# Attention on one Trainium2 core: two score chunks of a unit next to each other in TensorE's order

## The chip, the cores and the metric

The kernel runs on one core of one Trainium2 chip. The metric is the time of one execution on the device, in microseconds (us). A core has five engines with a queue each: TensorE (PE; PEld are its weight loads), VectorE (DVE), ScalarE (ACT), GpSimd (POOL) and SyncE (SP), which here only issues transfers. Engines meet through semaphores.

## What is computed

A two-layer trunk over 1024 latent and 256 context tokens of width 1024. Layer 0 has grouped-query attention beside a bidirectional RWKV-7, layer 1 differential attention; each layer ends in a mixture of experts. The edit is in the attention, which is in the reference:

```python
def gqa_attend(q, k, v):
    s = jnp.einsum('bqhgd,bkhd->bhgqk', q, k, preferred_element_type=jnp.float32) * HEAD_DIM ** -0.5
    p = jax.nn.softmax(s, axis=-1).astype(v.dtype)
    return jnp.einsum('bhgqk,bkhd->bqhgd', p, v)

def diff_attend(q, k, v, lam):
    s = jnp.einsum('bqhcd,bkhcd->bhcqk', q, k, preferred_element_type=jnp.float32) * HEAD_DIM ** -0.5
    pr = jax.nn.softmax(s, axis=-1)
    pr = pr[:, :, 0] - lam * pr[:, :, 1]
    return jnp.einsum('bhqk,bkhe->bqhe', pr.astype(v.dtype), v)
```

## The kernel before

The kernel is a sequence of phases; each ends in a barrier of all engines. `attn_phase` is used twice: with the tag al for grouped-query attention and with ad for differential attention. Its work is cut into units. A unit is a pair of heads (of maps, in the differential case) and one tile of 128 queries against nk tiles of 128 keys. Differential attention has 64 units, all with nk = 10. Grouped-query attention has 40: for each of 4 pairs 8 latent units with nk = 10, then 2 context units with nk = 2.

A unit goes through these steps:

- `score(n, i)`, TensorE, L703: chunk i of the scores of unit n, up to 512 keys wide, for both heads of the pair. A unit with nk = 10 has chunks of 512, 512 and 256 (below: score 0, 1 and 2), one with nk = 2 has one of 256. There are two pairs of PSUM banks `S`, and the chunks of the whole phase take them in turn: a score waits until DVE has evicted the score two before it (`s_out`).
- `take`, DVE, L777: evicts a chunk from both banks into `p` and takes its maximum; `maximum` (L782) follows the last chunk of a unit.
- `exponent`, ACT, L826: the exponential over the whole row, one for each of the two heads, in the iteration after the unit's scores.
- `combine`, DVE, L789 to L794, differential only: subtracts the two maps, two iterations after the scores.
- `turn(m, i)`, TensorE, L715: transposes group i, four tiles of `p`, into one of two banks `tr`. A differential unit has 10 tiles and so 3 groups (4, 4 and 2 tiles); a grouped-query unit has 20 tiles and 5 groups, a context unit 4 tiles and 1 group.
- `copy_out`: copies a group from `tr` to `pT` in SBUF. In the differential case ACT does all of them (L848). In the grouped-query case ACT does groups 0, 2 and 4 and DVE (L753) groups 1 and 3.
- `values(m, i)`, TensorE, L726: multiplies group i with V. The copied group is the stationary operand, so its weight load waits for the copy.
- `output`, ACT, L836 to L842: scales and stores the result.

The loop on each engine runs over iterations n and takes up unit n for the first steps and an older unit m for the later ones: m = n - 3 in the differential case, m = n - 2 in the other. The order within an iteration is written out for each engine. On ACT it is: copy 0, exponential 0, copy 1, exponential 1, the other copies, output. On DVE: first chunk, `combine`, other chunks, `maximum`, and in the grouped-query case a copy after each of the first two chunks. On TensorE it is the loop that the edit changes: at each step i it puts a score if the share of scores put is behind the share of steps gone, then `turn(m, i)`, then `values(m, i - 1)`.

Of the kernel before, what the change touches and what calls it, by code (L numbers as in the profile page):

```python
# [620 lines left out]
def attn_phase(nc, sems, tag, d, qT, kT, k_tiles, kmap, V, out, units, pairs, q_from, diff):  # L621

    LAG = 3 if diff else 2
    RING = 4
    U = len(units)
    WMAX = max(nk for _, _, nk in units) * P
    VW = P if diff else HD
    LAMBDA_INIT = 0.8 - 0.6 * math.exp(-0.3)

    def chunks(n):  # L630
        W = units[n][2] * P
        return [(a, min(512, W - a)) for a in range(0, W, 512)]

    def groups(n):
        nk = units[n][2]
        cols = [(c, kt) for c in range(1 if diff else 2) for kt in range(nk)]
        return [cols[a:a + 4] for a in range(0, len(cols), 4)]
# [6 lines left out]
    def turned_out(eng, g, ev_act, ev_dve):  # L644

        if on_act[g]:
            eng.wait_ge(ev_act, act_until[g + 1])
        else:
            eng.wait_ge(ev_dve, g + 1 - act_until[g + 1])

    with ExitStack() as ctx:
# [22 lines left out]
        with nc.Block() as block:  # L674
            @block.sync
            def _(sp):
                sp.dma_start(ident[:, :], d["ident"]).then_inc(const_in, 16)
                for i in range(pairs):
                    if i < k_tiles:
                        sp.dma_start(K[:, i, :], kT[i * P:(i + 1) * P, :]).then_inc(k_in[i], 16)  # L680
                    sp.dma_start(q[:, i, :], qT[i * P:(i + 1) * P, q_from:TOK]).then_inc(q_in[i], 16)
                    if i == 0 and diff:
                        for j, n in enumerate(("od_lq1", "od_lk1", "od_lq2", "od_lk2")):
                            sp.dma_start(lqk[:, j, :], d[n].to_broadcast([P, HD])).then_inc(const_in, 16)
                for v in range(2):
                    sp.wait_ge(o_out[v], 16 * ((U + 1 - v) // 2))

            @block.tensor
            def _(pe):
                pe.wait_ge(const_in, 16 * (5 if diff else 1))  # L690

                def score(n, i):
                    pair, t, nk = units[n]
                    if i == 0:
                        pe.wait_ge(q_in[pair], 16)
                        pe.wait_ge(k_in[kmap(pair)], 16)
                    a, w = chunks(n)[i]
                    j = chunk0[n] + i
                    if j >= 2:
                        pe.wait_ge(s_out, 2 * (j - 1))  # L700
                    for c in range(2):
                        h = slice(c * HD, (c + 1) * HD)
                        x = nc.tensor.matmul(S[j % 2][c][:, 0:w], q[h, pair, t * P - q_from:(t + 1) * P - q_from], K[h, kmap(pair), a:a + w], start=True, stop=True)  # L703
                    x.then_inc(s_done, 1)

                def turn(m, i):
                    g = group0[m] + i
                    if g >= 2:
                        turned_out(pe, g - 2, ev_act, ev_dve)
                    if diff:  # L710
                        pe.wait_ge(mixed, m + 1)
                    else:
                        pe.wait_ge(p_done, 2 * m + groups(m)[i][-1][0] + 1)
                    for k, (c, kt) in enumerate(groups(m)[i]):
                        x = nc.tensor.transpose(tr[g % 2][:, k * P:(k + 1) * P], p[:, m % RING, c, kt * P:(kt + 1) * P], ident[:, :])  # L715
                    x.then_inc(tr_done, 1)

                def values(m, i):
                    pair, t, nk = units[m]
                    g = group0[m] + i  # L720
                    turned_out(pe, g, ev_act, ev_dve)
                    if i == 0 and m >= 2:
                        pe.wait_ge(o_done, m - 1)
                    for k, (c, kt) in enumerate(groups(m)[i]):
                        vc = pair * P if diff else kmap(pair) * HD
                        x = nc.tensor.matmul(acc[m % 2][:, c * HD:c * HD + VW], pT[:, g % 3, k * P:(k + 1) * P], V[:, kt, vc:vc + VW], start=kt == 0, stop=kt == nk - 1)  # L726
                    x.then_inc(pv_done, 1)

                for n in range(U + LAG):
                    m = n - LAG  # L730
                    G = len(groups(m)) if m >= 0 else 0
                    C = len(chunks(n)) if n < U else 0
                    put = 0
                    for i in range(max(G + 1, C)):
                        if put < C and put * (G + 1) <= i * C:
                            score(n, put)
                            put += 1
                        if i < G:
                            turn(m, i)
                        if 1 <= i <= G:  # L740
                            values(m, i - 1)
                    while put < C:
                        score(n, put)
                        put += 1
# [1884 lines left out]
```

## Time and profile before

| | us |
|---|---|
| median of 3 runs | 5791.07 |
| lowest, highest | 5783.55, 5791.42 |
| the profiled execution | 5788.05 |
| its span | 5785.7 |
| TensorE busy in the span | 4182.2 (72%) |
| DVE busy | 2196.7 (38%) |
| ACT busy | 1422.0 (25%) |

The profiled execution lasts 2.35 us longer than its span, the time around the first and the last instruction. The grouped-query loop lies between about 660 and 1010 us of the span, the differential one between about 4190 and 4655. The busy shares are means over many phases; for this change only the two loops count. In the rows below, "idle before" tells how long an engine stood before an instruction and what released it. The trace shows a matmul of float32 operands as two records, a transpose as one; so a score of one chunk for two heads is x4, and values of four tiles are x8.

### The profile page before, as it was taken

The page shows a single profiled execution, that of the slowest core. Times are in us where ns is not written, and L with a number is a line of the kernel's source. Part 1 is how long each engine was busy: PE and PEld are TensorE (multiplying, and loading weights), DVE is VectorE, ACT ScalarE, POOL GpSimd, SP SyncE. Part 2 cuts the span into 40 slices and gives each one's busy share as a digit, 9 for nine tenths or more (in the row PEclk, how much of TensorE's full clock was granted, in tenths as well). Part 3 has the DMA queues.
Part 4 walks back from the last instruction along what each step waited for, and adds up shares of the span by engine and source line. Part 5 has one row for each costly group of instructions (what it writes and reads, how often), then busy time and mean ns, then how long its engine had stood idle before and what let it go on. Part 6 is the DMA issues. An engine that isn't in the chain of part 4 may idle for free. (4 is left out here: it accounts for less than half of the span.)

```text
span 5785.7 us, 71070 instructions
## 1 busy us (share of the span) xinstructions
PE 4182.2 (72%) x23474; PEld 2739.1 (47%) x23475; DVE 2196.7 (38%) x4254; ACT 1422.0 (25%) x3188; POOL 639.3 (11%) x1135
## 2 busy tenths in 40 slices
PE   5597599395876949574499983598199955497893
PEld 1385377284765838453133321487056644132331
DVE  0312544666556656624000002411677733200003
ACT  0210254343333424212011110210056622011111
POOL 0000000131322313300100002000300010100001
PEclk9798799697988969786799996799599977799997
DMA  9421100101010010133886697322510023799943
GB/s 336 147 86 68 62 9 9 38 1 25 10 25 10 0 34 1 46 128 109 312 339 235 228 377 282 118 89 76 193 49 10 11 98 105 274 364 397 374 165 145
DMA packets 350063, 778.83 MB, mean 135 GB/s; under 512 B 52000, under 2 KB 95284, under 8 KB 349796
## 3 DMA queue, kind: packets, MB, share of 16 engines
q1 hardware_dynamic: 297640, 624.64, 30.1%
q10 hardware_dynamic: 37696, 103.04, 4.6%
q0 software_dynamic: 14544, 48.79, 2.4%
q8 instruction: 105, 1.72, 0.1%
q14 instruction: 78, 0.64, 0.0%
HBM read 656.45 MB, written 122.58 MB: 135 GB/s over the span
## 5 line engine op out<-in xcount | busy, mean ns | idle before, releaser
L2306 PE MATMUL ex_bG<-ex_w,ex_xT 128*64 x880 | 424.7, 639 | 134.5 <-SPq L2227 77.3
L2306 PE MATMUL ex_bY<-ex_w,ex_aT 128*64 x880 | 392.6, 599 | 74.5 <-DVE ex_aT L2369 59.7
L2309 PE MATMUL ex_bG<-ex_w,ex_xT 128*64 128x512 f32 x880 | 424.7, 639 | 0.0
L367 PE MATMUL p_acc<-hT,p_wh 128*128 128x512 f32 (+1 forms) x1056 | 376.2, 356 | 24.6 <-DVE p_wl L379 24.6
L2309 PE MATMUL ex_bY<-ex_w,ex_aT 128*64 128x512 f32 x880 | 392.8, 600 | 0.0
L2306 PE MATMUL ex_bU<-ex_w,ex_xT 128*64 x880 | 386.6, 592 | 0.0
L2309 PE MATMUL ex_bU<-ex_w,ex_xT 128*64 128x512 f32 x880 | 386.6, 592 | 0.0
L2367 DVE TENSOR_TENSOR ex_a<-ex_sg,ex_bU 128x512 f32<-128x512 f32 x55 | 37.9, 688 | 917.9 <-PE ex_bU L2309 917.9
L367 PE MATMUL p_acc<-hT_rest,p_wh 128*128 128x512 f32 (+1 forms) x1056 | 375.7, 356 | 0.0
L367 PE MATMUL p_acc<-hT,p_wl 128*128 128x512 f32 (+1 forms) x1056 | 375.2, 355 | 0.0
L2306 PEld LDWEIGHTS ex_bG<-ex_w,ex_xT 128*64 128x64 f32 x880 | 127.9, 148 | 415.3 <-issue 415.3
L703 PE MATMUL ad_S<-ad_K,ad_q 64*128 64x512 f32 (+1 forms) x768 | 193.5, 584 | 125.2 <-DMA ad_lqk<-in_od_lk 120.8
L2306 PEld LDWEIGHTS ex_bY<-ex_w,ex_aT 128*64 128x64 f32 x880 | 116.7, 138 | 306.5 <-issue 306.5
L777 DVE TENSOR_SCALAR_CACHE_REDUCE ad_p<-ad_S 128x512 f32<-128x512 f32 (+1 forms) x384 | 215.7, 600 | 100.5 <-PE ad_S L703 100.5
L2306 PEld LDWEIGHTS ex_bU<-ex_w,ex_xT 128*64 128x64 f32 x880 | 120.6, 137 | 248.7 <-issue 248.7
L388 DVE COPY p_o<-p_acc 128x512 f32<-128x512 f32 x88 | 49.1, 558 | 469.5 <-PE p_acc L367 468.7
L367 PEld LDWEIGHTS p_acc<-hT,p_wh 128*128 128x128 f32 x1056 | 200.9, 190 | 53.9 <-issue 25.4
L1354 PE MATMUL rs_bankZ<-rs_X,rs_Bm 128*128 128x128 f32 x1280 | 224.7, 277 | 0.0
L1351 PE MATMUL rs_bankY<-rs_ident,rs_X 128*128 128x128 f32 x640 | 185.1, 289 | 47.3 <-DVE rs_Bm L1558 39.0
L367 PEld LDWEIGHTS p_acc<-hT_rest,p_wh 128*128 128x128 f32 x1056 | 201.0, 190 | 27.9
L367 PEld LDWEIGHTS p_acc<-hT,p_wl 128*128 128x128 f32 x1056 | 200.6, 190 | 28.2
L1450 ACT ACTIVATE rs_Y<-rs_bankY 128x256 f32<-128x256 f32 x320 | 122.4, 384 | 350.3 <-PE rs_bankZ L1354 350.2
(362 smaller groups left out, 8841.4 us busy)
## 6 DMA issues: line engine op xcount, KB each, us to landing
ex_w<-in_moe_w_gate SPq DMA_DIRECT2D x64, 2048.0 KB, 17.8
ex_w<-in_moe_w_up SPq DMA_DIRECT2D x64, 2048.0 KB, 21.2
ex_w<-in_moe_w_down SPq DMA_DIRECT2D x64, 2048.0 KB, 18.1
mods_w<-in_mod_w SPq DMA_DIRECT2D x24, 2048.0 KB, 13.0
projT_dram<-p_o ACTq DMA_DIRECT2D x44, 640.0 KB, 2.9
yb_dram<-ex_y ACTq DMA_DIRECT2D x55, 512.0 KB, 6.3
p_w<-in_od_w_in SPq DMA_DIRECT2D x12, 1024.0 KB, 5.1
n_x<-x_dram SPq DMA_DIRECT2D x20, 512.0 KB, 4.1
```

Of the source, the lines that this page charges most:

```text
L367: mm = nc.tensor.matmul(acc[u % 2][c][:, 0:n], a[:, u // 2, k, at], b[:, k, t0:t0 + n], start=k == 0 and x == 0, stop=k == KT - 1 and x == 2)
L388: nc.vector.tensor_copy(o[:, u % 2, t0:t0 + n], acc[u % 2][c][:, 0:n]).then_inc(dve_ev, 1)
L703: x = nc.tensor.matmul(S[j % 2][c][:, 0:w], q[h, pair, t * P - q_from:(t + 1) * P - q_from], K[h, kmap(pair), a:a + w], start=True, stop=True)
L777: nc.vector.tensor_scalar(p[:, u, c, a:a + w], S[j % 2][c][:, 0:w], 1.0, None, ALU.mult, ALU.max, accum_out=top[:, u, c, i:i + 1]).then_in ...
L1351: nc.tensor.transpose(bankY[g][:, dr * P:(dr + 1) * P], X[:, g, dr, :], ident[:, :])
L1354: x = nc.tensor.matmul(to, Bm[:, g, dr, l, :], X[:, g, dr, :], start=True, stop=True)
L1450: aa.did(f"X{g}" if l == 1 else f"Y{l}{g}", nc.scalar.activation(to[:, g, :, :], bankY[g][:, 0:256].rearrange("p (d t) -> p d t", d=2), AC ...
L2306: nc.tensor.matmul(bank[0:BR, :], stationary[:, k, 0:BR], w[:, ds(slot0 + (offset + k * n), 512)], start=k == 0, stop=k == tiles - 1)
L2309: m = nc.tensor.matmul(bank[BR:P, :], stationary[:, k, BR:P], w[:, at:at + 512], start=k == 0, stop=k == tiles - 1)
L2367: nc.vector.tensor_tensor(a[:, :], sg[:, :], bU[:, :], ALU.mult).then_inc(a_done, 1)
```

## The change

One condition puts a score; the change lets it put up to two in a row, chunk `put` and the one after it, as far as the unit has them. The count `put` rises by two, so the condition holds again only later. All other engines keep their order.

```diff
                     for i in range(max(G + 1, C)):
                         if put < C and put * (G + 1) <= i * C:
-                            score(n, put)
-                            put += 1
+                            for _ in range(min(2, C - put)):
+                                score(n, put)
+                                put += 1
                         if i < G:
                             turn(m, i)
                         if 1 <= i <= G:
                             values(m, i - 1)
```

In the rows that follow, one line is what stands on TensorE in a row with the same names: ad_S and al_S are scores, ad_tr and al_tr transposes, ad_acc and al_acc values, and the number at the end counts matmuls. In the differential loop, TensorE, one iteration before:

```order
L703 MATMUL ad_S<-ad_K,ad_q 128x512 x2
L715 MATMUL ad_tr<-ad_ident,ad_p 128x128 x8
L726 MATMUL ad_acc<-V,ad_pT 128x128 x4
L703 MATMUL ad_S<-ad_K,ad_q 128x512 x2
L715 MATMUL ad_tr<-ad_ident,ad_p 128x128 x2
L726 MATMUL ad_acc<-V,ad_pT 128x128 x4
L703 MATMUL ad_S<-ad_K,ad_q 128x256 x2
L726 MATMUL ad_acc<-V,ad_pT 128x128 x2
```

and after:

```order
L703 MATMUL ad_S<-ad_K,ad_q 128x512 x4
L715 MATMUL ad_tr<-ad_ident,ad_p 128x128 x8
L726 MATMUL ad_acc<-V,ad_pT 128x128 x4
L715 MATMUL ad_tr<-ad_ident,ad_p 128x128 x2
L726 MATMUL ad_acc<-V,ad_pT 128x128 x4
L703 MATMUL ad_S<-ad_K,ad_q 128x256 x2
L726 MATMUL ad_acc<-V,ad_pT 128x128 x2
```

Score 1 has moved from behind values 0 to the place right behind score 0 (x4), and between values 0 (the first ad_acc row) and values 1 (the second) only the two transposes of group 2 are left.

In the grouped-query loop, TensorE, an iteration with two latent units, before:

```order
L703 MATMUL al_S<-al_K,al_q 128x512 x2
L715 MATMUL al_tr<-al_ident,al_p 128x128 x8
L726 MATMUL al_acc<-V,al_pT 128x64 x4
L703 MATMUL al_S<-al_K,al_q 128x512 x2
L715 MATMUL al_tr<-al_ident,al_p 128x128 x4
L726 MATMUL al_acc<-V,al_pT 128x64 x4
L715 MATMUL al_tr<-al_ident,al_p 128x128 x4
L726 MATMUL al_acc<-V,al_pT 128x64 x4
L703 MATMUL al_S<-al_K,al_q 128x256 x2
L715 MATMUL al_tr<-al_ident,al_p 128x128 x4
L726 MATMUL al_acc<-V,al_pT 128x64 x8
```

and after:

```order
L703 MATMUL al_S<-al_K,al_q 128x512 x4
L715 MATMUL al_tr<-al_ident,al_p 128x128 x8
L726 MATMUL al_acc<-V,al_pT 128x64 x4
L715 MATMUL al_tr<-al_ident,al_p 128x128 x4
L726 MATMUL al_acc<-V,al_pT 128x64 x4
L715 MATMUL al_tr<-al_ident,al_p 128x128 x4
L726 MATMUL al_acc<-V,al_pT 128x64 x4
L703 MATMUL al_S<-al_K,al_q 128x256 x2
L715 MATMUL al_tr<-al_ident,al_p 128x128 x4
L726 MATMUL al_acc<-V,al_pT 128x64 x8
```

Score 1 has moved ahead of the transposes of groups 0 and 1; behind values 0 the transposes of group 2 follow at once. The place of score 2 is as it was.

In the grouped-query loop, TensorE, an iteration in which unit n is a latent one and the older unit m a context one, with a single group, before (five rows):

```order
L703 MATMUL al_S<-al_K,al_q 128x512 x2
L715 MATMUL al_tr<-al_ident,al_p 128x128 x4
L703 MATMUL al_S<-al_K,al_q 128x512 x2
L726 MATMUL al_acc<-V,al_pT 128x64 x4
L703 MATMUL al_S<-al_K,al_q 128x256 x2
```

and after, with the first scores of the next iteration as its last row:

```order
L703 MATMUL al_S<-al_K,al_q 128x512 x4
L715 MATMUL al_tr<-al_ident,al_p 128x128 x4
L726 MATMUL al_acc<-V,al_pT 128x64 x4
L703 MATMUL al_S<-al_K,al_q 128x256 x2
L703 MATMUL al_S<-al_K,al_q 128x512 x4
```

Score 1 has moved from between the transposes and the values of the group to a place ahead of both.

## Rows read from the trace of the kernel before

**Rows 1.** Busy time by stretch: steady differential loop, then its tail.

```profile
core 0: us, PE busy (x) PEld busy (x) DVE busy (x) ACT busy (x) POOL busy (x), PEclk, DMA share, GB/s
4209.00:4640.41 431.41, 416.30 (x2557) 267.93 (x2558) 329.06 (x972) 268.53 (x487) 0.00 (x0) 1.00 0.04 10
4640.41:4655.50 15.09, 11.58 (x93) 10.24 (x91) 4.40 (x11) 8.45 (x17) 0.00 (x0) 1.00 0.05 14
```

**Rows 2.** Waits of TensorE's weight loads, 4209 to 4640: total, times, longest.

```profile
PEld ad_acc L726 <- ACT ad_pT L848: 29.6, 61, 0.5
```

**Rows 3.** Order of time, one differential unit: start, duration, engine, line, operation, tiles, count.

```profile
4399.67 1.13 PE L703 MATMUL ad_S<-ad_K,ad_q 64*128 64x512 f32 x4
...
4400.73 0.86 PEld L715 LDWEIGHTS ad_tr<-ad_ident,ad_p 128*128 128x128 f32 x8 [0.76 <-issue]
...
4401.42 0.60 ACT L848 ACTIVATE ad_pT<-ad_tr 128x512 f32<-128x512 f32 x1 [1.28 <-PE ad_tr L715]
...
4402.07 0.97 PEld L726 LDWEIGHTS ad_acc<-V,ad_pT 128*128 128x128 f32 x8 [0.49 <-ACT ad_pT L848]
...
4403.16 1.13 PE L703 MATMUL ad_S<-ad_K,ad_q 64*128 64x512 f32 x4
...
4403.26 0.59 ACT L848 ACTIVATE ad_pT<-ad_tr 128x512 f32<-128x512 f32 x1
...
4404.39 0.97 PEld L726 LDWEIGHTS ad_acc<-V,ad_pT 128*128 128x128 f32 x8
...
4405.09 0.38 ACT L848 ACTIVATE ad_pT<-ad_tr 128x256 f32<-128x256 f32 x1
...
4405.48 0.70 PE L703 MATMUL ad_S<-ad_K,ad_q 64*128 64x256 f32 x4
...
4406.11 0.71 PE L726 MATMUL ad_acc<-V,ad_pT 128*128 128x128 f32 x4
...
4406.58 0.42 DVE L777 TENSOR_SCALAR_CACHE_REDUCE ad_p<-ad_S 128x256 f32<-128x256 f32 x1
...
4406.76 1.13 PE L703 MATMUL ad_S<-ad_K,ad_q 64*128 64x512 f32 x4
```

**Rows 4.** Order of time, behind the last score of the differential loop.

```profile
4641.56 0.60 ACT L848 ACTIVATE ad_pT<-ad_tr 128x512 f32<-128x512 f32 x1 [0.47 <-PE ad_tr L715]
...
4642.21 0.97 PEld L726 LDWEIGHTS ad_acc<-V,ad_pT 128*128 128x128 f32 x8 [0.89 <-ACT ad_pT L848]
...
4643.40 0.58 ACT L848 ACTIVATE ad_pT<-ad_tr 128x512 f32<-128x512 f32 x1
...
4644.04 0.97 PEld L726 LDWEIGHTS ad_acc<-V,ad_pT 128*128 128x128 f32 x8 [0.69 <-ACT ad_pT L848]
...
4647.89 0.97 PEld L726 LDWEIGHTS ad_acc<-V,ad_pT 128*128 128x128 f32 x8 [0.89 <-ACT ad_pT L848]
...
4649.00 1.08 PEld L726 LDWEIGHTS ad_acc<-V,ad_pT 128*128 128x128 f32 x9
```

**Rows 5.** Order of time, grouped-query values 0 and 1: latent iteration, then context-scoring one.

```profile
671.53 1.10 PE L726 MATMUL al_acc<-V,al_pT 128*128 128x64 f32 x8 [0.25 <-ACT al_pT L848]
...
674.12 1.00 PE L726 MATMUL al_acc<-V,al_pT 128*128 128x64 f32 x8
...
817.72 0.69 DVE L753 COPY al_pT<-al_tr 128x512 f32<-128x512 f32 x1 [0.24 <-PE al_tr L715]
...
817.93 1.10 PE L726 MATMUL al_acc<-V,al_pT 128*128 128x64 f32 x8 [0.25 <-ACT al_pT L848]
...
819.32 1.00 PE L726 MATMUL al_acc<-V,al_pT 128*128 128x64 f32 x8
```

**Rows 6.** Order of time, grouped-query, the older unit a context one.

```profile
832.64 0.42 PEld L715 LDWEIGHTS al_tr<-al_ident,al_p 128*128 128x128 f32 x4 [0.76 <-issue]
...
834.28 0.97 PEld L726 LDWEIGHTS al_acc<-V,al_pT 128*128 128x128 f32 x8 [0.76 <-ACT al_pT L848]
...
835.32 1.67 PE L703 MATMUL al_S<-al_K,al_q 64*128 64x256 f32 x8
...
836.92 0.42 PEld L715 LDWEIGHTS al_tr<-al_ident,al_p 128*128 128x128 f32 x4 [0.76 <-issue]
```

## The prediction

> **What bounds the kernel now.** I read the busy table by stretch first, since the edit touches only the attention phases, and of them the two loops that print as al_ (grouped-query) and ad_ (differential). In the steady part of the differential loop TensorE is busy 416.30 of 431.41 us at a granted clock of 1.00 [rows 1]: its own order of work sets the pace, DVE (329.06) and ACT (268.53) have slack in the sum, and no transfer is in the way. Next the waits of its weight loads: the values wait for ACT's copies once per unit, 29.6 us in 61 times, 0.49 each [rows 2]. Then one unit in the order of time [rows 3], where the reader should follow three things.
>
> First, TensorE's period: score 0 of one unit at 4399.67, of the next at 4406.76, so 7.09 us. Its pieces are score 0 to transposes 1.06 (to 4400.73), transposes of groups 0 and 1 until values 0 can load 1.34 (to 4402.07), values 0 to score 1 1.09 (to 4403.16), values 0 to score 2 in all 3.41 (to 4405.48), score 2 to values 2 0.63, and values 2 to the next score 0 0.65. Second, ACT's chain: copy of group 0 at 4401.42 (0.69 after the transposes' start), copy of group 1 at 4403.26, 1.84 later, because an exponential over 1280 elements is queued between them, and copy of group 2 at 4405.09, 3.67 after the first. Third, the margin: copy 1 ends at 4403.85 and values 1 loads at 4404.39. Values 1 never waits, with 0.54 us to spare, because score 1 (1.06) stands between values 0 and it. Phases end in a barrier, so what the loops gain or lose goes into the time undiminished.
>
> **The change part by part.** No matmul, eviction or exponential is added or removed, and each of the 91 pairs that now stands together is the same two scores: 61 in the differential loop, 24 in grouped-query iterations whose older unit is a latent one (5 groups), 6 in those whose older unit is a context one (1 group). The first iterations of each loop, the last ones, and the 8 in which a context unit is scored keep their order. Only TensorE's order changes; the lists of DVE, ACT, SP and POOL stay, so no queue is moved past and no transfer starts from a moved step.
>
> Two scores in a row. The trace has one warm pair, a score of 256 followed by one of 512: 835.32 to 836.92, 1.60 us [rows 6], where apart they take 0.63 + 1.06 = 1.69 [rows 3]. So a pair saves 0.09, and two of 512 take 2.12 - 0.09 = 2.03, an estimate. The bounds are a saving of 0 and, there being no other warm pair, of 0.2 (twice the row and a little): 91 x 0.09 = 8 us more, or 91 x 0.11 = 10 us less. I take the row. What a pair of 512 puts ahead of the transposes is thus 2.03 - 1.06 = 0.97 us.
>
> Differential loop, 61 units. Transposes start 2.03 after score 0 instead of 1.06. Values 0 follow 1.34 later as before, for they wait for ACT's copy 0 in either order. Then comes the point of the whole sum: between values 0 and values 1 stand only two transposes. After its last score the loop runs in just that order, and there, with the exponential still between the copies, values 0 load at 4642.21 and values 1 at 4644.04: 1.83 us, since copy 1 starts at 4643.40, again 1.84 after copy 0 at 4641.56 [rows 4]. Two units later, with no exponential left, the same stretch takes 4647.89 to 4649.00, 1.11 us [rows 4]. The wait is 0.72 us, and it is new in the steady part. From values 1 to score 2 it is 1.09, as from values 0 to score 1 in [rows 3]; then 0.63 and 0.65. New unit: 2.03 + 1.34 + 1.83 + 1.09 + 0.63 + 0.65 = 7.57 us, 0.48 more than 7.09. Over 61 units: **+29.3 us**. Values 2 could wait too: copy 2 ends 4.05 after copy 0's start, which makes 4.79 after the transposes' start with the hand-over, and values 2 come at 1.34 + 1.83 + 1.09 + 0.63 = 4.89. It is 0.1 clear.
>
> The new reader of a buffer is score 1: it writes the one in which the unit before left its score 2, and now comes one score after score 0. DVE's second eviction of that started at 4406.58 and took 0.42, so 1.52 after score 2's start [rows 3]; the new score 1 comes 0.63 + 0.65 + 0.97 = 2.25 after it. It has 0.73 us, no wait. Behind it on TensorE would stand the transposes, and so ACT's whole chain. The order of DVE (two evictions, then 1.55 of combining) lets score 1 sit in its bank for longer than before; that costs nothing, as score 2 uses the other bank and the next user of this one is the score 0 of the next unit, over 5 us later.
>
> Grouped-query loop, 24 full iterations. Here copy 1 is DVE's, not queued behind an exponential. Before, values 0 to values 1 takes 671.53 to 674.12, 2.59, with score 1 within. An iteration that scores a context unit already runs the order without it: 817.93 to 819.32, 1.39, with DVE's copy at 817.72 done long before [rows 5]. So 2.59 becomes 1.39, and 0.97 is added in front: -0.23 each, **-5.5 us**. The later copies keep their place or get more room.
>
> Grouped-query loop, 6 iterations with a context unit behind. Its only group is transposed at 832.64 and its values load at 834.28, 1.64 later, score 1 having filled the time of the copy [rows 6]. Without that cover they can load 1.34 after the transposes (the copy of 512 elements as in [rows 3]), and they start 0.97 later: 0.97 - 0.30 = +0.67 each, **+4.0 us**.
>
> The sum: 29.3 - 5.5 + 4.0 = +27.8 us. The profiled execution took 5788.05 (span 5785.7), which gives 5815.8. The median of the runs shown is 5791.07, 3.0 above it; I put the forecast between the two sums, at **5817**.
>
> On the pair, rows and a rule differ. In rows, transposes after a score load their weights only as they start themselves: the load at 4400.73 stands where the next stage begins [rows 3]. The Trainium skill, "TensorE: Matmul & The Clock Gate" (Step-by-step: what each phase is for), says that TensorE's queue may pull a weight load ahead of matmuls in flight. By that rule a score followed by transposes would lose nothing and pairing scores would save nothing, and the result would be some 8 us later, 5825; by the row it is 5817. I go by the row.
>
> **The rivals.** Values 1 doesn't wait, and the fewer turns of kind win: the differential unit is 1.83 - 1.11 = 0.72 shorter than my sum, 6.85, and so 0.24 below the present one. That makes -14.6 - 5.5 + 4.0 = -16 us, 5772. For it speaks only that TensorE is the busiest engine; against it, that ACT's order is fixed in the program and that the tail shows the wait. It would need copy 1 to come 0.7 us earlier. Chance 0.05.
>
> The wait is there but smaller, because score 1's place or ACT's hand-over shifts some tenths: a stall of 0.4 instead of 0.72 gives 61 x 0.16 = 10 less 1.5, +8 us, 5796. Chance 0.07. That the edit doesn't do what it says can be left out: TensorE's list has 91 rows fewer, one for each pair.
>
> Much slower by the S banks: if DVE's eviction of score 2 ended over 0.73 us later than I reckon, score 1 would wait each time. At 1.2 us later that is 0.5 x 61 = 30 us on top, 5847. DVE's 76% busy share speaks for some danger, its wait for score 2 in every unit against. Chance 0.03.
>
> Much slower by the clock. The granted clock is 1.00 (2.4 GHz) in the steady part with one short wait per unit, and also in the tail of 15.09 us, with TensorE busy 11.58 [rows 1]. A drop to 1.2 GHz over a tenth of the loop would double 43 us of its work and give 5860. The Trainium skill, "TensorE: Matmul & The Clock Gate" (A second HAM failure mode: psum-queue depth-cycling), tells of a kernel whose short idle times between groups made the clock swing; the tail's row disagrees. Chance 0.03.
>
> **How the numbers follow.** My case has 0.82; with the pair's bounds (+8, -10) and the 8 us by which the runs of before spread, it lies between 5803 and 5830. The range goes a little toward the others, 5799 to 5833, and leaves out about 2 in 10. A measurement tells about 0.2%, 11.6 us, from no change. Faster by more: 0.05. Within it: 0.08, the smaller stall and what is left of my own low end. Slower: 0.87.
>
> **What would show it.** The differential period should read 7.57 us: transposes 2.03 after score 0, values 1 marked as waiting for ACT's copy 61 times at some 0.7 us, total near 44 us. ACT's copies stay 1.84 apart. Score 1 waits for nothing. The grouped-query stretch from values 0 to values 1 falls from 2.59 to 1.39. If values 1 wait for nothing, step one of the sum is wrong; if score 1 waits for DVE, the bank is; if the period fits and the time doesn't, something outside the two loops moved.

## The result, and the profile after

The changed kernel takes 5800.74 us in the median (5790.87 to 5811.0, 20 runs), the kernel before 5786.05 (5779.82 to 5792.91, 20 runs): a ratio of 1.0024, 95% interval [1.0017, 1.0031], 14.7 us or 0.24% slower [9.8 to 17.9 us]. The forecast was 5817, some 28 us slower. The direction and the mechanism came as foretold, the size is about half.

The same unit of the differential loop in the trace after, in the order of time (start, duration, engine, line, operation, tiles, count); it answers to [rows 3]. The lines of the code behind the edit have moved by one.

```profile
4399.33 0.42 DVE L778 TENSOR_SCALAR_CACHE_REDUCE ad_p<-ad_S 128x256 f32<-128x256 f32 x1
...
4399.51 1.99 PE L703 MATMUL ad_S<-ad_K,ad_q 64*128 64x512 f32 x8
...
4400.04 0.19 PEld L703 LDWEIGHTS ad_S<-ad_K,ad_q 64*128 64x128 f32 x2 [0.24 <-DVE ad_p L778]
...
4401.42 0.86 PEld L715 LDWEIGHTS ad_tr<-ad_ident,ad_p 128*128 128x128 f32 x8 [0.76 <-issue]
...
4402.12 0.60 ACT L849 ACTIVATE ad_pT<-ad_tr 128x512 f32<-128x512 f32 x1 [2.14 <-PE ad_tr L715]
...
4402.77 0.97 PEld L726 LDWEIGHTS ad_acc<-V,ad_pT 128*128 128x128 f32 x8 [0.49 <-ACT ad_pT L849]
...
4403.96 0.59 ACT L849 ACTIVATE ad_pT<-ad_tr 128x512 f32<-128x512 f32 x1
...
4404.60 0.97 PEld L726 LDWEIGHTS ad_acc<-V,ad_pT 128*128 128x128 f32 x8 [0.69 <-ACT ad_pT L849]
...
4405.69 0.70 PE L703 MATMUL ad_S<-ad_K,ad_q 64*128 64x256 f32 x4
...
4406.96 1.99 PE L703 MATMUL ad_S<-ad_K,ad_q 64*128 64x512 f32 x8
```

The unit lasts 4406.96 - 4399.51 = 7.45 us instead of 7.09. The new wait is where it was foretold: values 1 stand 0.69 us for ACT's second copy, which starts 1.84 after the first (4403.96 against 4402.12), as in [rows 3] and [rows 4]. From values 0 to values 1 it is 1.83, from there to score 2 1.09, both as summed. What differs is the pair: from score 0 to the transposes 1.91 us, not 2.03. Score 1 waits for nothing: the eviction that it needs ends at 4399.75 (the first row), and its weights load at 4400.04. The label "DVE" on that load is wrong, for its releaser had long been done; the margin is 0.29 us.

The waits of the weight loads over 4194 to 4640 (engine and line, what they waited for, us in total, times, longest) answer to [rows 2]:

```profile
PEld ad_acc L726 <- ACT ad_pT L849: 90.4, 180, 0.7
```

29.6 us in 61 waits has become 90.4 in 180, three for each of 60 units: 0.49 + 0.69 + 0.33. The last is the time that values 2 always stand behind score 2 (0.33 in the trace of before too, there put down to "issue"), so the new one is 0.69.

The grouped-query loop, a latent iteration and an iteration with a context unit behind it, which answer to [rows 5] and [rows 6]:

```profile
805.84 1.99 PE L703 MATMUL al_S<-al_K,al_q 64*128 64x512 f32 x8
...
807.76 1.09 PE L715 MATMUL al_tr<-al_ident,al_p 128*128 128x128 f32 x8
...
809.10 1.11 PE L726 MATMUL al_acc<-V,al_pT 128*128 128x64 f32 x8 [0.25 <-ACT al_pT L849]
...
810.49 1.00 PE L726 MATMUL al_acc<-V,al_pT 128*128 128x64 f32 x8
...
815.72 0.70 PE L703 MATMUL al_S<-al_K,al_q 64*128 64x256 f32 x4
...
833.26 0.65 PE L715 MATMUL al_tr<-al_ident,al_p 128*128 128x128 f32 x4
...
834.60 1.10 PE L726 MATMUL al_acc<-V,al_pT 128*128 128x64 f32 x8 [0.69 <-ACT al_pT L849]
...
836.74 0.42 DVE L778 TENSOR_SCALAR_CACHE_REDUCE al_p<-al_S 128x256 f32<-128x256 f32 x1
...
837.22 0.30 PEld L703 LDWEIGHTS al_S<-al_K,al_q 64*128 64x128 f32 x4 [0.85 <-DVE al_p L778]
...
838.28 0.42 PEld L715 LDWEIGHTS al_tr<-al_ident,al_p 128*128 128x128 f32 x4 [0.76 <-issue]
```

Values 0 to values 1 take 1.39 us, as forecast, the pair 1.92, and the whole iteration 9.88 instead of 10.22. Behind a context unit values follow the transposes by 1.34 and stand 0.69 for the copy. The last rows are ones that I had not foreseen: there the scores 2, 0 and 1 stand in a row, and score 1 does wait for DVE's eviction of score 2, which ends at 837.16; its weights load at 837.22, and its first matmul comes about 0.2 us later than it would behind score 0 without a wait.

What is left is where the time went. Lengths of the stretches in every trace, in us, read from the first and last start of their tiles. "Loop" is from the first score to the last values; RWKV from the first of its four preparation phases to the readout; none of these kernels changes anything in RWKV. The kernels other than before and after are those of the experiments below.

| kernel | grouped-query loop | differential loop | RWKV | ratio of times [95%] |
|---|---|---|---|---|
| before | 349.0 | 464.0 | 1358.8 | |
| before, again | 349.1 | 464.0 | 1359.7 | |
| after | 344.9 | 485.1 | 1349.9 | 1.0024 [1.0017, 1.0031] |
| after, again | 344.9 | 485.4 | 1356.7 | 1.0038 [1.0025, 1.0052] |
| pairs in the differential loop only | 349.1 | 485.1 | 1354.9 | 1.0035 [1.0021, 1.0048] |
| pairs in the grouped-query loop only | 344.8 | 460.8 | 1364.3 | 0.9993 [0.9984, 1.0002] |
| pairs, ACT's copies first | 344.9 | 440.4 | 1360.3 | 0.9956 [0.9942, 0.9970] |
| ACT's copies first, no pairs | 349.0 | 463.0 | 1352.2 | 1.0000 [0.9991, 1.0009] |
| transposes first, ACT's copies first | 346.3 | 412.2 | 1357.8 | 0.9907 [0.9892, 0.9922] |
| pair of scores 1 and 2 | 344.8 | 439.8 | 1356.7 | 0.9954 [0.9940, 0.9967] |
| transposes first, both loops | 326.8 | 413.1 | 1358.5 | 0.9882 [0.9864, 0.9901] |
| transposes first, ACT as before | 344.9 | 411.6 | 1352.8 | 0.9911 [0.9895, 0.9927] |
| pairs, keys cut 256, 512, 512 | 344.8 | 509.3 | 1352.8 | 1.0075 [1.0057, 1.0093] |
| transposes first, keys cut 256, 512, 512 | 344.8 | 410.1 | 1349.2 | 0.9890 [0.9873, 0.9907] |

In the two loops the change costs 21.1 - 4.1 = +17.0 us, 0.29%; both intervals of the changed kernel hold that. (The unit alone gives 61 x 0.36 = +22 us for the differential loop. What is missing lies in its first units, which the next section comes to.)

### The profile page after: what moved, and what is told of

It reads as the page before. It is cut to its first block and busy times, and to the rows that moved or that the text cites. A ratio compares the mean times of both kernels' runs of the same rounds, so it can differ in the third digit from the quotient of the medians.

```text
span 5792.0 us, 71070 instructions
## 1 busy us (share of the span) xinstructions
PE 4155.1 (72%) x23474; PEld 2733.8 (47%) x23475; DVE 2189.4 (38%) x4254; ACT 1420.8 (25%) x3188; POOL 639.9 (11%) x1135
## 5 line engine op out<-in xcount | busy, mean ns | idle before, releaser
L703 PE MATMUL ad_S<-ad_K,ad_q 64*128 64x512 f32 (+1 forms) x768 | 175.8, 563 | 124.7 <-DMA ad_lqk<-in_od_lk 119.9
L726 PE MATMUL ad_acc<-V,ad_pT 128*128 128x128 f32 x1280 | 193.1, 290 | 45.7 <-ACT ad_pT L849 45.7
## 6 DMA issues: line engine op xcount, KB each, us to landing
ex_w<-in_moe_w_gate SPq DMA_DIRECT2D x64, 2048.0 KB, 17.9
```

## The experiments

**The changed kernel, and its halves.** The first question was whether the two loops are all. The edit of the halves:

```diff
-                            for _ in range(min(2, C - put)):
+                            for _ in range(min(2 if diff else 1, C - put)):
```

and for the other half `min(1 if diff else 2, C - put)`. Expected of the changed kernel again:

> The changed kernel again, to have it beside its halves on one chip. Loop theory: the differential loop is 21 us longer and the grouped-query loop 4 us shorter than before (464.0 to 485.1 and 349.0 to 344.9 from the first score to the last values in the two traces), and all other phases are the same but for scatter: +17 us. Rival, the change also moves later phases (the four RWKV phases together read 9 us shorter after the change): these phases are again 9 us shorter here, and the time is +8 to +15 us with them.

Of the differential half:

> Two scores in a row in the differential loop only. Loop theory: 61 units of 7.455 instead of 7.09 us, +22 us, loop length 485 us, grouped-query loop 349 us. Theory of the record, with 0.48 us a unit: +29 us. Rival, later phases moved by the change: under +17 us, with RWKV phases shorter than before.

Of the grouped-query half:

> Two scores in a row in the grouped-query loop only. Loop theory: -4 us (24 iterations shorter, 6 with a context unit behind longer), the grouped-query loop 345 instead of 349 us, the differential one 464. Theory of the record: -1.5 us. Rival, the pair costs here too: 0 or slower.

And of the kernel before, once more:

> The kernel before once more, for its trace alone. If the 9 us by which the RWKV phases differ between the two first traces are scatter, these phases differ by some us between this execution and the first one too; if the change made them, they are within 1 us of the first (1358.8 us from the first to the readout).

Measured: 5806.75, 5805.07 and 5781.53 us against 5785.18 before, so +21.6, +19.9 and -3.7; the kernel before, in a single run, 5786.11. The halves add up to +16.2. The -3.7 is not clear of noise by itself (the interval of its ratio holds 1); its loop is 4.2 us shorter.

Each loop has, to 0.4 us, the same length wherever it has the same order, but for three: this half's differential loop of 460.8, expected at 464; a grouped-query loop of 346.3 where 344.9 was due; and differential loops of 411.6 and 413.1 in two kernels with the same code there. The traces show where these differences lie: in the first units, ahead of the loop's first output, and in the clock. From the first output on, the steady units are equal to 0.01 us. The first 25 us of the differential loop, in the kernel before and in the half with 460.8:

```profile
core 0: us, PE busy (x) PEld busy (x) DVE busy (x) ACT busy (x) POOL busy (x), PEclk, DMA share, GB/s
4190.59:4215.59 25.00, 20.51 (x80) 9.89 (x82) 18.43 (x63) 9.91 (x17) 0.00 (x0) 0.74 0.74 300
4193.36:4218.36 25.00, 19.46 (x98) 10.11 (x98) 20.64 (x71) 11.82 (x19) 0.00 (x0) 0.94 0.79 320
```

TensorE stands idle for 121 us before the loop, and the loop starts at the lower of its two clock levels (granted clock 0.50 in the first 5 us of the kernel before, 1.2 GHz). How much of the first 25 us runs at the full clock differs from execution to execution: mean 0.74 in one, 0.94 in the other, whose loop is 3.2 us shorter. For the 346.3 it is 0.81 against 0.92 where the loop has 344.9, and for 413.1 against 411.6 it is 0.75 against 0.85.

The RWKV stretch was not shorter because of the change: it reads 1356.7 in the changed kernel's second trace, 1364.3 with pairs in one loop and 1352.2 in a kernel with none. In my two traces of before it happened to agree to 1 us, so my test by that alone would have pointed the wrong way; over all fourteen it scatters by 15 us with no order by kernel. It goes with the granted clock of the stretch: 0.868 in the longest, 0.877 in the shortest, and nearly in that order between (correlation -0.94 over the fourteen). Which of the two makes the other, no run here shows. It is this that makes a profiled span (5792.0 against 5785.7) a poor measure of 17 us.

**Is it the copy behind the exponential?** ACT's order in the differential loop, on top of the pairs:

```diff
-                    for c in range(2):
-                        if c < len(mine):
-                            copy_out(act, copy, ev_act, m, mine[c])
-                        if 0 <= n - 1 < U:
-                            exponent(n - 1, c)
-                    for i in mine[2:]:
-                        copy_out(act, copy, ev_act, m, i)
+                    if diff:
+                        for i in mine[0:2]:
+                            copy_out(act, copy, ev_act, m, i)
+                        if 0 <= n - 1 < U:
+                            exponent(n - 1, 0)
+                        for i in mine[2:]:
+                            copy_out(act, copy, ev_act, m, i)
+                        if 0 <= n - 1 < U:
+                            exponent(n - 1, 1)
+                    else:
...
```

> The changed kernel with ACT's order in the differential loop changed to copy 0, copy 1, exponential 0, copy 2, exponential 1: copy 1 no longer stands behind an exponential. Theory (values 1 wait for copy 1 behind the exponential, and that alone makes the pair a loss): the wait of 0.69 us on values 1 is gone, unit 7.455 - 0.72 - 0.10 = 6.63 us, -28 us against the kernel before in this loop and -4 in the other, -32 us in all. Rival (TensorE loses by the pair itself, by its banks or its weight loads): the unit stays above 7.09 and the time at or above that of before.

The same on the kernel before, without pairs:

> The kernel before, with ACT's new order alone and no pairs. Theory: nothing waited for copy 1 before, score 1 covered it, so the unit stays 7.09 us and the time within 2 us of before. Rival (ACT's order helps by itself, whatever TensorE does): a good part of the 30 us gain of the order shows here.

Measured: 5759.44 and 5782.87 us against 5783.05, so -23.6 and -0.2. In the first, over 410 us of the steady part, and two rows of a unit:

```profile
PEld ad_acc L726 <- ACT ad_pT L849: 30.1, 61, 0.9
```

```profile
4441.61 0.97 PEld L726 LDWEIGHTS ad_acc<-V,ad_pT 128*128 128x128 f32 x8 [0.49 <-ACT ad_pT L849]
...
4442.72 0.97 PEld L726 LDWEIGHTS ad_acc<-V,ad_pT 128*128 128x128 f32 x8
```

The 0.69 is gone (1.11 from values 0 to values 1), and the loop falls from 485 to 440 us. The unit is 6.73 us (4438.35 to 4445.08), 0.1 above what I expected: a stretch from values 1 to score 2 is 1.09 from the weight load, and I had counted 0.99. The gain in time was 8 us short of -32. Without pairs the same order gives nothing, as score 1 hid the copy: the unit stays at 7.09, and of the 1.0 us by which that loop is shorter 0.9 lie behind its last score, where copy 1 had no cover before. So the pair is not a loss in itself; what it uncovered is.

**A pair that leaves the cover in place.** ACT as before; TensorE's order in the differential loop written out:

```diff
+                    if diff and G and C:
+                        for step, i in (('s', 0), ('t', 0), ('t', 1), ('v', 0), ('s', 1), ('s', 2), ('t', 2), ('v', 1), ('v', 2)):
+                            (score if step == 's' else turn if step == 't' else values)(n if step == 's' else m, i)
+                        continue
```

> Changed kernel, but in the differential loop the pair is scores 1 and 2, behind values 0, and score 0 stands alone; ACT's order is that of before. Theory: score 1 covers copy 1 as before, so values 1 don't wait, and a score of 512 followed by another takes 0.85 instead of 1.06: unit 6.65 us, -27 us in this loop, -4 in the other, -31 us. If what a pair saves goes by the smaller of the two scores (0.09 for 256 and 512) the unit is 6.77 and the time -24 us. Rival (any pair loses): slower than before.

Measured: 5756.1 us against 5783.05, -27. The unit is 6.70 (4436.56 to 4443.26). From score 1 to the transposes of group 2 it takes 1.49, where apart it is 1.69.

**Pair and cover at once.** The same form with the order `t0, t1, s0, s1, v0, t2, v1, s2, v2`, and ACT's copies first:

> Changed kernel with ACT's new order, and on TensorE in the differential loop transposes 0 and 1, then scores 0 and 1, then values 0: the pair now covers copies 0 and 1. Theory: the wait of 0.49 us on values 0 goes too; unit 1.0 + 1.91 + 1.11 + 0.99 + 0.63 + 0.44 = 6.1 us, 60 us less than before in this loop and 4 in the other, -64 us. Rival (DVE becomes the bound, busy some 5.6 us a unit, with scores waiting for its evictions): unit 6.3 to 6.6, -34 to -52 us.

with ACT as before:

> As the run with transposes first in the differential loop, with ACT's order of before. Theory (copy 1 is late only where nothing but two transposes stands between values 0 and 1 after a late values 0; here copy 1 ends 3.1 us after the transposes' start, values 1 come at about 4.1, copy 2 at 4.8 against values 2 at 5.8): the unit is 6.27 us as with the new ACT order, time -54 us. Rival (ACT's order is needed for the gain): unit 6.6 to 6.9, -15 to -35 us.

and, with ACT as before, the grouped-query loop in that manner too: up to two groups transposed, up to two scores, values 0, then the rest as it was:

> Transposes first and the pair of scores behind them in both loops; every other engine's list is that of before, ACT's in the differential loop too. Theory: the pair covers the copies in the grouped-query loop as well, 0.4 to 0.5 us for each of some 38 iterations, less up to 4 us because DVE's copy 1 now stands behind a later eviction: grouped-query loop 330 to 337 us, -66 to -73 us against the kernel before. Rival (DVE's copy behind the eviction eats it all): grouped-query loop 345 us, -56 us.

Measured: 5729.42 us against 5783.05 (-53.6), 5726.2 against 5776.38 (-50.2), and 5709.59 against 5776.38 (-66.8). A unit with ACT as before:

```profile
4431.86 1.99 PE L703 MATMUL ad_S<-ad_K,ad_q 64*128 64x512 f32 x8
4431.93 0.60 ACT L853 ACTIVATE ad_pT<-ad_tr 128x512 f32<-128x512 f32 x1 [0.47 <-PE ad_tr L715]
...
4433.77 0.59 ACT L853 ACTIVATE ad_pT<-ad_tr 128x512 f32<-128x512 f32 x1
4433.77 0.97 PEld L726 LDWEIGHTS ad_acc<-V,ad_pT 128*128 128x128 f32 x8 [0.76 <-issue]
...
4434.88 0.97 PEld L726 LDWEIGHTS ad_acc<-V,ad_pT 128*128 128x128 f32 x8
```

Copy 1 still starts 1.84 after copy 0, behind its exponential, but ends at 4434.36, before values 1 come at 4434.88. The unit is 6.26 to 6.27 us with either order of ACT, and 6.1 was my sum, too low by 0.16: stage changes at which I had taken the shorter of two spacings. It isn't DVE's bound: in each unit DVE stands 0.93 us until the first score is there. With the grouped-query loop in that manner too, that loop has 326.8 us, below the 330 to 337 that I expected (9.41 us an iteration instead of 9.88), though the time of -66.8 is at the edge of what I said, -66 to -73. The best version is this last one, 1.2% faster than the kernel before.

**How much does a pair save?** My one row for it was a score of 256 followed by one of 512, saving 0.09, and every pair in the traces after saved 0.2. So I cut the keys of a differential unit the other way, on the changed kernel:

```diff
+        if diff:
+            return [(0, 256), (256, 512), (768, 512)]
         return [(a, min(512, W - a)) for a in range(0, W, 512)]
```

> The changed kernel with a differential unit's keys cut as 256, 512, 512 instead of 512, 512, 256: the pair is a small score and a large one, the single score is large. Theory (what a pair saves goes by its first score: 0.09 us behind one of 256, 0.21 behind one of 512, 0.20 in the pair of 512 and 256): unit 7.57 us, 0.11 above the changed kernel, +24 us against before. Rival (any warm pair saves 0.2, and the 0.09 of the trace of before belonged to its place): unit 7.45, +17 us.

Measured: 5823.91 us against 5776.38, +47.5, ratio 1.0075, and a unit of 7.86 us, which neither side expected:

```profile
4433.66 1.97 PE L705 MATMUL ad_S<-ad_K,ad_q 64*128 64x256 f32 x8
...
4433.76 0.69 DVE L780 TENSOR_SCALAR_CACHE_REDUCE ad_p<-ad_S 128x512 f32<-128x512 f32 x1
...
4434.51 0.30 PEld L705 LDWEIGHTS ad_S<-ad_K,ad_q 64*128 64x128 f32 x4 [0.54 <-DVE ad_p L780]
```

Score 1 waits for its bank: DVE's second eviction of the last score, now of 512, ends at 4434.45. It is the rival with the banks, which the real change does not meet in this loop; here it is real, and it hides what I wanted to see. The run settled nothing on pairs. So the same cut with the transposes between the last score and the next pair:

> Transposes first in the differential loop (ACT's order of before), with a unit's keys cut as 256, 512, 512. Now the transposes stand between a unit's last score and the next pair, so score 1 need not wait for DVE as it did in the run that cut the keys so without them. Theory (a pair saves 0.09 us behind a score of 256 and 0.2 behind one of 512): score 0 to values 0 takes 1.60 us, unit 6.37, 0.11 us above the 6.26 of the same order with 512, 512, 256, so +7 us against that run and -47 against before. Rival (any pair saves 0.2 and the row of the trace of before held a wait of its own): 1.48 and 6.26, -54 us.

```profile
4425.00 1.56 PE L705 MATMUL ad_S<-ad_K,ad_q 64*128 64x256 f32 x8
...
4425.32 0.41 PEld L705 LDWEIGHTS ad_S<-ad_K,ad_q 64*128 64x128 f32 x4
...
4426.49 0.97 PEld L728 LDWEIGHTS ad_acc<-V,ad_pT 128*128 128x128 f32 x8 [0.76 <-ACT ad_pT L855]
...
4428.69 1.13 PE L705 MATMUL ad_S<-ad_K,ad_q 64*128 64x512 f32 x4
```

Measured: 5719.84 us against 5788.52, and 1.49 us from the small score to the values, so a saving of 0.2 behind a score of 256 too; the unit is 6.26 (the row at 4428.69 was at 4422.43 a unit earlier). The -68.7 us are more than the -54 of the rival and the -58 that the two loops give; the interval holds -58. The rival won: the row of before held a wait of its own. It can be found there, in the trace of before:

```profile
835.02 0.69 DVE L777 TENSOR_SCALAR_CACHE_REDUCE al_p<-al_S 128x512 f32<-128x512 f32 x1
...
835.83 0.33 PEld L703 LDWEIGHTS al_S<-al_K,al_q 64*128 64x128 f32 x4 [0.21 <-issue]
```

The second score of that pair is score 0 of the next unit. It writes the bank of score 1, whose second eviction ended at 835.71, and its weights load 0.12 later, 0.51 behind the small score's start, where in the clean pair above they load 0.32 behind it (4425.32 against 4425.00). That pair is 0.11 us shorter, 1.49 against 1.60. What follows, transposes there and values here, makes no such difference: with two scores of 512 it is 1.91 before either. The view put the idle time down to "issue". No run takes this wait away in its own place; it is read from these times.

## Why the prediction was right and wrong

- *The bound.* Right. TensorE's order sets the pace of both loops, and what they gain or lose is in the time: the halves give +19.9 and -3.7 us for loops of +21.1 and -4.2, though the second is not clear of noise.
- *The exposed copy, 61 times.* Right in place, count and size: 0.69 seen, 0.72 said, read from the tail of the loop, which ran in the new order already [rows 4]. (The row without an exponential there is of the next unit, not of one two units later; its 1.11 us stands.) Taking the copy from behind the exponential removes it and turns +22 into -24 us, each against before; the same edit without pairs gives nothing.
- *Two scores in a row.* This is the step that failed: the term was mis-sized. The prediction put a pair at 0.09 us saved, from [rows 6], and kept 0.2 as the bound. It is 0.21: the pair takes 1.91 to 1.92, not 2.03. 91 x 0.12 = 11 us, and 27.8 - 11 = 17, the measured cost of the loops. That it comes out so evenly is partly luck: with the pair put right the sum is +22.0 and -5.1 for the two loops, and they measured +21.1 and -4.1. Of the 16 us between 5817 and 5800.74, 11 are this term, 3 are the base (the sum stood on 5789.2, where 20 runs give 5786.05), and the other 2 are within noise. The row was the nearest, but it was not clean: it was 0.11 us longer than the same pair without a wait for DVE, as the last experiment shows. What was said of one order of sizes was really that of one bank.
- *The weights pulled ahead.* The alternative by the Trainium skill, "TensorE: Matmul & The Clock Gate" (Step-by-step: what each phase is for), with no saving by a pair at all, missed further than my row. Between two scores the weights of the second do load early: at 4400.04, 0.53 after the first began, while its own first matmul stands at 4400.47, 0.96 after. Before transposes the load still begins with them, 0.76 idle. The trace agrees with the rule between scores and not from a score to transposes; why, no run here shows.
- *The grouped-query loop.* -5.5 + 4.0 = -1.5 said, -4.1 measured. 24 x 0.34 = -8.2 for the latent iterations, of which 0.12 each is the pair again. The six behind a context unit cost 0.74 each, +4.4 (5.02 us from 833.26 to 838.28, where it was 4.28 from 832.64 to 836.92); the remaining -0.3 lies at the end of the loop. Said was 0.67, so near by luck, for the parts are others: a cheaper pair, and a wait for the bank that I had checked in the differential loop only.
- *The banks.* Right that score 1 doesn't wait in the differential loop, but the slack there is 0.29 us and not 0.73: the sum reckoned with score 1's first matmul (4400.47), while its weights load already at 4400.04, and they need the bank free too, as the load at 4434.51 right behind an eviction shows. It was wrong to leave the other loop out. The run with the small chunk first shows what it costs when the slack is used up: 7.86 instead of 7.45 us.
- *The clock.* The granted clock stayed at 1.00 (2.4 GHz) over 4194 to 4644, the new waits and all. The short idle times between groups of which the Trainium skill, "TensorE: Matmul & The Clock Gate" (A second HAM failure mode: psum-queue depth-cycling), tells did not lower it here. It is below 1.00 only in the first units of the loop, before as after.

The 20 runs give 14.7 us where the loops give 17; the rest is within the interval (9.8 to 17.9).

## What to carry to other kernels

Before two matmuls of a kind are put together, ask what the one that moves was hiding: here 1.06 us of score 1 covered a copy that another engine had queued behind an exponential. The tail of a software pipeline can already run in the order that an edit would bring to its middle; here it priced the new wait to 0.03 us. A row taken as a price must be clean: look at what released the instruction, in every bank that it writes, before multiplying it by 91.

## What the runs showed that I had not expected

- A score (512 columns, two heads) takes 1.06 us up to transposes or values, and adds 0.85 to a pair (1.91 in all); 0.2 us are saved by each pair that waits for no bank, in each of the three combinations of sizes that ran (1.49 for 512 and 256 in either order, against 1.69 apart).
- The same pair that costs 17 us saves 50 when it stands between transposes and values (the grouped-query loop has the same pairs in both, so the difference is of the differential loop alone): the place in the order is worth more than the pair.
- An idle time marked "issue" can hide a wait for a bank (835.83, 0.12 us behind the end of the eviction), and one marked "DVE" can be none (4400.04, 0.29 us behind it).
- Phases without a difference in code scatter by 15 us between executions (RWKV 1349.2 to 1364.3), while the two loops repeat within 0.4 us, with three exceptions of 1.4 to 3.2. Both go with the granted clock: of the stretch in RWKV, and of the first 25 us in the loops, which start at 1.2 GHz.
